# The second feed-forward's input product by seven half-size products per pair of weight tiles

## The reference, cut to what matters

```python
D_FF_2 = -(-8 * D_MODEL // (3 * 256)) * 256          # 2816 = 22 tiles of 128

def swiglu(hn, w_ffn_in, w_ffn_out):
    gate, up = jnp.split(hn @ w_ffn_in, 2, axis=-1)
    return (jax.nn.silu(gate) * up) @ w_ffn_out
...
        h = h + swiglu(rmsnorm(h, norm_ffn_gain[l]), w_ffn_in[l], w_ffn_out[l])
```

## Time and profile before

| | us |
|---|---|
| median of 3 runs | 2235.63 |
| lowest, highest | 2234.02, 2238.86 |
| profiled execution, its own time | 2232.78 |
| its span (first to last instruction) | 2231.0 |
| PE busy / PEld busy | 2164.0 (97%) / 1686.8 (76%) |
| DVE busy | 1110.3 (50%) |
| ACT busy | 790.7 (35%) |
| POOL busy | 118.3 (5%) |
| mean granted TensorE clock | 0.986 of full |

### The profile page before, as it was taken

The page is one execution under the profiler, slowest core; times in us unless marked ns, Lnnn a source line. Parts: engine busy times, 40 slices in busy tenths (PEclk is TensorE's granted clock), DMA queues, the critical chain, the costliest instruction groups (busy, mean ns, idle before and its releaser), DMA issues. The chain is left out here.

```text
span 2231.0 us, 32534 instructions
## 1 busy us (share of the span) xinstructions
PE 2164.0 (97%) x13484; PEld 1686.8 (76%) x13484; DVE 1110.3 (50%) x1775; ACT 790.7 (35%) x1252; POOL 118.3 (5%) x131
## 2 busy tenths in 40 slices
PE   8999889999999999989999999999999999999999
PEld 6676557888888989977666888667666678888887
DVE  4464775777733467654346444346432354444422
ACT  4332464444422453322224222225455433222211
POOL 1000242000000000000000000000012101000000
PEclk9999899999999999989999999999999999999999
DMA  4224002222222344322115421115711132222222
GB/s 175 76 71 147 1 1 85 95 95 95 95 94 95 104 146 153 109 85 71 58 58 176 139 87 59 58 62 190 245 67 43 57 100 88 93 95 93 95 94 95
DMA packets 76290, 214.45 MB, mean 96 GB/s; under 512 B 8432, under 2 KB 12912, under 8 KB 76144
## 3 DMA queue, kind: packets, MB, share of 16 engines
q1 hardware_dynamic: 76144, 212.37, 28.5%
HBM read 183.64 MB, written 27.66 MB: 95 GB/s over the span
## 5 line engine op out<-in xcount | busy, mean ns | idle before, releaser
L297 PE MATMUL ps<-nx_hi,whi 128*128 128x264 f32 (+1 forms) x1504 | 533.9, 355 | 13.7 <-DVE nx_lo L377 9.3
L282 DVE TENSOR_TENSOR wlo<-raw,whi 128x1024 fp32r<-128x1024 f32 x282 | 347.2, 1231 | 332.0 <-ACT whi L275 331.6
L299 PE MATMUL ps<-nx_hi,wlo 128*128 128x264 f32 (+1 forms) x1504 | 509.9, 339 | 0.0
L298 PE MATMUL ps<-nx_lo,whi 128*128 128x264 f32 (+1 forms) x1504 | 509.4, 339 | 0.0
L275 ACT ACTIVATE whi<-raw 128x1024 fp32r<-128x1024 f32 x282 | 298.4, 1058 | 587.1 <-PE ps L299 420.2
L297 PEld LDWEIGHTS ps<-nx_hi,whi 128*128 128x128 f32 x1504 | 284.7, 189 | 75.6 <-issue 32.8
L299 PEld LDWEIGHTS ps<-nx_hi,wlo 128*128 128x128 f32 x1504 | 284.9, 189 | 32.1
L298 PEld LDWEIGHTS ps<-nx_lo,whi 128*128 128x128 f32 x1504 | 285.3, 190 | 30.0 <-issue 1.9
L299 PE MATMUL ps<-x_hi,wlo 128*128 128x512 f32 x528 | 209.5, 397 | 0.0
L298 PE MATMUL ps<-x_lo,whi 128*128 128x512 f32 x528 | 208.3, 394 | 0.0
L297 PE MATMUL ps<-x_hi,whi 128*128 128x512 f32 x528 | 208.1, 394 | 0.0
(11 more groups left out here) (468 smaller groups left out, 2872.3 us busy)
## 6 DMA issues: line engine op xcount, KB each, us to landing
raw<-stream_dram SPq DMA_DIRECT2D x285, 512.0 KB, 3.5
qk_spill<-ring SPq DMA_DIRECT2D x16, 264.0 KB, 2.1
qk_cols<-qk_spill SPq DMA_DIRECT2D x16, 264.0 KB, 5.2
v_spill<-ring SPq DMA_DIRECT2D x16, 264.0 KB, 2.1
v_cols<-v_spill SPq DMA_DIRECT2D x16, 264.0 KB, 4.4
dz_spill<-ring SPq DMA_DIRECT2D x16, 256.0 KB, 2.1
dz<-dz_spill SPq DMA_DIRECT2D x16, 256.0 KB, 4.4
sbk_spill<-ring SPq DMA_DIRECT2D x8, 264.0 KB, 2.1
```

Source lines behind the costliest of these rows:

```text
L282: dve.tensor_tensor(K.wlo[:, n % HL], K.raw[:, n % RAW], K.whi[:, n % HL].bitcast(F32), ALU.subtract).then_inc(K.s_lo, 1)
L297: pe.matmul(out, whi, xhi, start=start, stop=False, skip_group_check=skip)
L298: pe.matmul(out, whi, xlo, start=False, stop=False, skip_group_check=skip)
L299: return pe.matmul(out, wlo, xhi, start=False, stop=stop, skip_group_check=skip)
```

## The change

The last stage gets a function of its own, `out_swiglu`. Three pairs (gate tile and up tile, p = 0 to 2, `PLAIN`) are computed as before. The other 19 (`SEVEN`) are each treated as a 2x2 block product: the weight's blocks are a11 (gate, k-tiles 0 to 3), a12 (gate, k-tiles 4 to 7), a21 (up, 0 to 3), a22 (up, 4 to 7), each [128, 512]; the activation's blocks are k-tiles 0 to 3 or 4 to 7 by tokens 0 to 255 or 256 to 511. Winograd's form of Strassen's scheme makes the four result blocks out of seven products of 4 k-tiles x 256 tokens, where the plain way takes eight.

- **Operands.** POOL makes four sums of weight blocks per pair (`weight_sums`: s1 = a21+a22, s2 = s1-a11, s3 = a11-a21, s4 = a12-s2; 128x512 each) into one buffer of four. The seven operands, in PE's order a11, s2, s3, a12, s1, a22, s4 (`o` = 0 to 6), are each split by ACT (`operand_hi`) and DVE (`operand_lo`) into seven half-chunk slots, one for each `o`; the slot is refilled for pair t+1 as soon as PE has done product `o` of pair t (`op_used`). Pairs arrive in four raw buffers, two of them laid over constants and parameters no longer needed.
- **Activation sums.** t1 to t4 are made once, by DVE, from `h` during pairs 0 and 1 and split by ACT and DVE during pair 1; `first_halves` is one ACT copy more.
- **Results.** PE accumulates the seven products in four banks, two sets of four by turns. Between products DVE and ACT add up results (u2, u3, u6, u7), because a12, a22 and s4 accumulate onto banks whose first product has to be read out before: PE waits for `u2` ahead of o=3, `u3` ahead of o=5, `u7` ahead of o=6.
- **The gated product** (L618's) moves from DVE to POOL (`gated`).
- **Activation tiles** are kept in float32 (`act`) and all split late: seven during the last pair, the other 15 during the first output of `w_ffn_out`. The first three chunks of `w_ffn_out` are split during the last pair.

Core of the diff:

```diff
--- before.py
+++ after.py
+PLAIN = 3
+SEVEN = FT - PLAIN
+QUARTER = 512
+OPERANDS = ("a11", "s2", "s3", "a12", "s1", "a22", "s4")
+SUMS = ("s1", "s2", "s3", "s4")
...
+        r, w = (self.first + o // 2) % HL, slice(QUARTER * (o % 2), QUARTER * (o % 2) + QUARTER)
+        return K.whi[:, r, w], K.wlo[:, r, w]
+    def part(self, t, name):
+        if name in SUMS:
+            return self.sums[:, SUMS.index(name)]
+        r, w = (2 * t + (name == "a22")) % 4, slice(QUARTER * (name != "a11"), QUARTER * (name != "a11") + QUARTER)
+        return self.raw[r][:, w]
...
+    def bank(self, t, o):
+        return 4 * ((t + 1) % 2) + (0, 1, 2, 0, 3, 2, 3)[o]
+    def out(self, t, o):
+        return self.K.ps[:, self.bank(t, o), 0:SEQ // 2]
...
+                for t in range(SEVEN):
+                    if t == 0:
+                        pe.wait_ge(z["factor_made"], 1)
+                    elif t == 1:
+                        pe.wait_ge(z["silu"], PLAIN)
+                        pe.wait_ge(z["act_full"], PLAIN)
+                    else:
+                        pe.wait_ge(z["both_scaled"], t - 1)
+                    for o, name in enumerate(OPERANDS):
+                        pe.wait_ge(z["op_lo"], 7 * t + o + 1)
+                        if t == 0 and name in ("s2", "s3", "s1", "a22"):
+                            pe.wait_ge(z["t_lo"], ("s2", "s3", "s1", "a22").index(name) + 1)
+                        if name in ("a12", "a22", "s4"):
+                            pe.wait_ge(z[{"a12": "u2", "a22": "u3", "s4": "u7"}[name]], t + 1)
+                        hi, lo = V.slot(o)
+                        for k in range(4):
+                            xh, xl = V.x[o][k]
+                            mm = three(pe, V.out(t, o), hi[:, k * P:(k + 1) * P], lo[:, k * P:(k + 1) * P], xh, xl,
+                                       k == 0 and name in ("a11", "s2", "s3", "s1"), k == 3, True)
+                        mm.then_inc(z["op_used"], 1)
+                pe.wait_ge(z["both_scaled"], SEVEN - 1)
...
+            def last_pair(o, tile, chunk):
+                if o in (1, 3, 5):
+                    chunk(down0 + o // 2)
+                if o == 0:
+                    tile(0)
+                    tile(1)
+                elif o != 5:
+                    tile(o + 1 if o < 5 else o)
+            @block.scalar
...
+                def operand_hi(t, o):
+                    if t > 0:
+                        act.wait_ge(z["op_used"], 7 * (t - 1) + o + 1)
+                    elif o < 6:
+                        act.wait_ge(K.s_used, down0 - HL + o // 2 + 1)
+                    V.ready(act, z, t, OPERANDS[o])
+                    act.activation(V.slot(o)[0], V.part(t, OPERANDS[o]), ACT.Copy).then_inc(z["op_hi"], 1)
...
+                def silu(t):
+                    gp = g[:, (PLAIN + t) % 2]
+                    act.wait_ge(z["both_scaled"], t + 1)
+                    act.activation(gp, gp, ACT.Silu).then_inc(z["silu_of_seven"], 1)
...
+                for t in range(SEVEN):
+                    if t >= 2:
+                        act.wait_ge(z["both_scaled"], t - 1)
+                    act.wait_ge(z["op_used"], 7 * t + 1)
+                    act.activation(V.u2[:, t % 2], V.out(t, 0), ACT.Copy).then_inc(z["first_part"], 1)
+                    for o in range(7):
+                        if o == 1 and t >= 1:
+                            silu(t - 1)
+                        if t + 1 < SEVEN:
+                            operand_hi(t + 1, o)
+                        else:
+                            last_pair(o, tile_hi, whole_hi)
+                silu(SEVEN - 1)
+                for f in range(7, 14):
+                    tile_hi(f)
+                for _, kind, i in ends:
+                    if kind == 0:
+                        whole_hi(down0 + i + HL)
+                        for f in range(14, 19) if i == 0 else range(19, FT) if i == 1 else ():
+                            tile_hi(f)
+            @block.gpsimd
+            def _(pool):
+                def weight_sums(t):
+                    a11, a12, a21 = V.part(t, "a11"), V.raw[2 * t % 4][:, QUARTER:], V.raw[(2 * t + 1) % 4][:, 0:QUARTER]
+                    a11, a12, a21 = V.part(t, "a11"), V.raw[2 * t % 4][:, QUARTER:], V.raw[(2 * t + 1) % 4][:, 0:QUARTER]
+                    a22 = V.part(t, "a22")
+                    s1, s2, s3, s4 = [V.part(t, n) for n in SUMS]
+                    V.ready(pool, z, t, "a11")
+                    V.ready(pool, z, t, "a22")
+                    for name, y, a, b, op in (("s1", s1, a21, a22, ALU.add), ("s2", s2, s1, a11, ALU.subtract),
+                                              ("s3", s3, a11, a21, ALU.subtract), ("s4", s4, a12, s2, ALU.subtract)):
+                        if t > 0:
+                            pool.wait_ge(z["op_lo"], 7 * (t - 1) + OPERANDS.index(name) + 1)
+                        if name in ("s2", "s4"):
+                            pool.wait_ge(z["weight_sums"], 4 * t + (1 if name == "s2" else 2))
+                        pool.tensor_tensor(y, a, b, op).then_inc(z["weight_sums"], 1)
+                def gated(t):
+                    y = act_[:, PLAIN + t]
+                    pool.wait_ge(z["up_scaled"], t + 1)
+                    pool.wait_ge(z["silu_of_seven"], t + 1)
+                    pool.tensor_tensor(y, y, g[:, (PLAIN + t) % 2], ALU.mult).then_inc(z["gated"], 1)
+                for d in range(1, KT):
+                    pool.wait_ge(z["squares"], d + 1)
+                    if d >= 2:
+                        pool.wait_ge(z["summed"], d - 1)
+                    pool.tensor_tensor(acc, acc, sq[:, d % 2], ALU.add).then_inc(z["summed"], 1)
+                for t in range(min(3, SEVEN)):
+                    weight_sums(t)
+                for t in range(SEVEN):
+                    gated(t)
+                    if t + 3 < SEVEN:
+                        weight_sums(t + 3)
+            @block.vector
+            def _(dve):
...
+                def operand_lo(t, o):
+                    dve.wait_ge(z["op_hi"], 7 * t + o + 1)
+                    hi, lo = V.slot(o)
+                    dve.tensor_tensor(lo, V.part(t, OPERANDS[o]), hi.bitcast(F32), ALU.subtract).then_inc(z["op_lo"], 1)
...
+                    dve.tensor_tensor(act_[:, p], act_[:, p], g[:, p % 2], ALU.mult).then_inc(z["act_full"], 1)
+                    if up0 + 2 * p + 1 + HL < down0:
+                        whole_lo(up0 + 2 * p + 1 + HL)
+                    if p == 0:
+                        dve.wait_ge(z["first_halves"], 1)
+                        for x, y, a, cols in ((t1, b11, 0, slice(MID, SEQ)), (t2, t1, 4, slice(MID, SEQ)), (t4, t2, 4, slice(0, MID))):
+                            for k in range(4):
+                                last = dve.scalar_tensor_tensor(x[:, k], K.h[:, a + k, cols], gain_ffn[:, a + k:a + k + 1], y[:, k],
+                                                                ALU.mult, ALU.subtract)
+                            if a == 0 or cols.start > 0:
...
+                for t in range(SEVEN):
+                    y, u2, gp = act_[:, PLAIN + t], V.u2[:, t % 2], g[:, (PLAIN + t) % 2]
+                    def spare(o):
+                        if t + 1 < SEVEN:
+                            operand_lo(t + 1, o)
+                        else:
+                            last_pair(o, tile_lo, whole_lo)
+                    spare(0)
+                    dve.wait_ge(z["op_used"], 7 * t + 2)
+                    dve.wait_ge(z["first_part"], t + 1)
+                    dve.tensor_tensor(u2, u2, V.out(t, 1), ALU.add).then_inc(z["u2"], 1)
+                    spare(1)
+                    dve.wait_ge(z["op_used"], 7 * t + 3)
+                    dve.wait_ge(z["u2"], t + 1)
+                    dve.tensor_tensor(y[:, MID:], u2, V.out(t, 2), ALU.add).then_inc(z["u3"], 1)
+                    spare(2)
+                    if t >= 2:
+                        dve.wait_ge(z["gated"], t - 1)
+                    elif t == 1:
+                        dve.wait_ge(z["act_full"], PLAIN)
+                    dve.wait_ge(z["op_used"], 7 * t + 4)
+                    dve.tensor_tensor(gp[:, 0:MID], V.out(t, 3), rs[:, 0:MID], ALU.mult)
+                    spare(3)
+                    dve.wait_ge(z["op_used"], 7 * t + 5)
+                    dve.wait_ge(z["u3"], t + 1)
+                    dve.tensor_tensor(y[:, MID:], y[:, MID:], V.out(t, 4), ALU.add).then_inc(z["u7"], 1)
+                    spare(4)
+                    dve.wait_ge(z["op_used"], 7 * t + 6)
+                    dve.tensor_tensor(y[:, 0:MID], u2, V.out(t, 5), ALU.add).then_inc(z["u6"], 1)
+                    spare(5)
+                    dve.wait_ge(z["op_used"], 7 * t + 7)
+                    ch.link(dve, dve.tensor_tensor(gp[:, MID:], u2, V.out(t, 6), ALU.add))
+                    dve.tensor_tensor(gp[:, MID:], gp[:, MID:], rs[:, MID:], ALU.mult).then_inc(z["both_scaled"], 1)
+                    spare(6)
```

(41 more changed lines are left out.)

208 lines of the change are left out of this document (added).

## The result

| | us |
|---|---|
| before, median of 4 runs | 2234.82 (2230.54 to 2238.86) |
| changed, median of 4 runs | 2282.07 (2279.39 to 2287.40) |
| ratio | 1.0216, 95% interval 1.0195 to 1.0237 |
| changed, profiled execution: own time, span | 2279.39, 2277.8 |

The account below looks back on a forecast made before the run. PE's matmul columns bound the kernel; changed pairs would wait on a 12.1 us loop. Terms 2.3 + 1.6 + 14.7 + 0.6 + 1.0 = +20.2 us gave 2253, plus 2.8 for the median: 2255, range 2231 to 2272.

Parts of the forecast that it names:

- PE's own time: 19 pairs: 84 matmuls of 256 columns at 0.118 us, 9.9 us per pair against 11.2 before, if PE never waited.
- The passage: POOL's tensor_tensor and DVE instructions with both inputs in SBUF hold one passage in turn; wanted 10.3 us per pair.
- Rival B: DVE keeps the passage between instructions, so s3 and s4 follow lo(0); pairs about 11.1 us, total about 2239; chance 0.16.
- The loop from lo(4) to u2: From product o=4 through the next pair's u2: 12.1 us per pair, PE pausing some 2.2 us ahead of o=3.
- rival C: Conflict real but not deciding, u2 seen under 4.2 us after PE's start; pairs 9.9 us, total 2215; chance 0.16.
- Pair 0, last pair, `w_ffn_out`: The ends of the stage: pair 0 takes 13.5 us (+2.3), the last pair 11.8 (+0.6), `w_ffn_out` +1.0.
- The clock: PE's granted clock in the stage: nothing in the forecast's sum; a tenth less, +5 us, only within the worse rival.
- rival D: Worse: gated product ahead of lo(0) or u7 late, 13.3 us pairs, 2274; or a tenth less clock, +5 us; chance 0.12.

## Why the prediction was wrong in size and right in mechanism

- **PE's own time** (0.118 us per matmul, 9.9 us per pair): right; 0.118 and 9.9 were measured with POOL out of the way. The Trainium skill's figure ("TensorE: Matmul & The Clock Gate", "Back-to-back issue gap"), 109 ns, would give 9.2; the measurement decides.
- **The passage**: right, from the ten rows, all from other stages. The Trainium skill, page "SBUF — State Buffer", section "Who interferes with whom", says that a DVE instruction with two SBUF inputs contends with a GpSimd instruction that reads SBUF and not with one that only writes it; the traces agree in both points (1.55 us beside sums, 0.69 beside writes). Rival B is out: POOL does get its turn between two such DVE instructions (s3 between gp*rs and lo(6), s4 between y*rs and lo(0)). One sign did not come: POOL's tensor_tensor was to take mostly 1.8 us and more; its groups have means of 1.30 to 1.70.
- **The loop from lo(4) to u2**: 12.1 us forecast, 12.4 measured with the pause filled and in the three pairs in which the clock stayed up; the pause 2.2 forecast, 2.2 measured; u2 seen 6.5 us after PE's start on the pair (6.4 laid out), which puts rival C out. Over pairs 1 to 17 the difference makes 4 us. (In the forecast's own sum 16 x 0.9 is 14.4 and not 14.7.)
- **Pair 0, last pair, `w_ffn_out`**: in pair 0 u2 was seen 7.7 us after PE's start (7.9 forecast), and the pair took 15.0 us. In three runs in which the clock stayed up behind the same pause it took 13.7 (13.5 forecast). The last pair took 11.7 (11.8), `w_ffn_out` 1.4 us more (1.0).
- **The clock** is the step that failed. The sum of the forecast held nothing for it. Only rival D named it, at 5 us in all: a tenth less clock over the whole pair, 1 us, of which two products' share, 0.3 us, was to lie in the loop. The average was right (0.90 over the stretch), but the clock does not fall by a tenth all along. It halves for 3.4 us at the pause, and these 3.4 us lie in o=3 and o=4, the very products that are in the loop. So nearly all of the loss counts: a pair with a fall takes 13.8 to 13.9 us, one without 12.4. Pair 0 lost 1.4 us and 14 of the 17 after it 20.7: 22 us where D had 5. Filling the pause in pairs 1 to 17 gave 19 of them back.

Sum: 20.2 forecast + 4 (loop) + 22 (clock) + 0.5 (pair 0 and `w_ffn_out`) = 46.7, against 46.6 us between the two profiled executions. What stays open is what decides whether the clock falls at a pause. Its length is not all: three of 18 pauses that look the same had no fall, and pair 0's of 3.5 us had one here and in four of the runs above, but none with u2 first, with the gated product on DVE, or with both.

## What to carry to other kernels

When work moves to POOL, list DVE's instructions with two SBUF inputs and lay both lists against each other up to the wait that PE hangs on; busy shares say nothing (DVE 88%, POOL 53% here). Then order DVE's list so that PSUM-reading instructions stand beside POOL's: with the same instructions that was worth 10 us. And when a forecast holds a pause of PE of a couple of microseconds, price the 3 us of work right behind it at the lower clock, for most of the pauses, and ask whether that work lies in the loop.

## What the runs showed of the hardware

- Of 18 PE pauses in the changed kernel (17 of 2.2 us, one of 3.5), with PE busy at full clock before each, 15 brought 3.4 us at 0.50 of the clock; 16 matmuls without use in the pause prevented it. With u2 first, 17 pauses of 1.3 us left the clock at 1.00.
- POOL's memset of 128x512 took 0.53 us and did not lengthen a DVE instruction with two SBUF inputs (54 overlaps, all 0.68 to 0.70 us); its tensor_tensor (1.30 us alone) did, by up to 1.1 us. DVE's instructions with an input in PSUM kept their length beside it (46 overlaps, 0.41 to 0.42 us on 256 columns).
